# Latent attention: the order of whole and 64-row score products on TensorE

## The reference

```python
def chunk_causal_mla_attention(q_nope, q_pe, k_nope, k_pe, v):   # 8 heads, per block of 128 queries
    s = (einsum('bqhd,bkhd->bhqk', qn_b, k_nope)      # 128 features of a head
         + einsum('bqhd,bkd->bhqk', qp_b, k_pe)) * scale   # 64 rotary features, one key for all heads
    s = where(chunk_mask(q_idx, k_idx), s, finfo.min)
    p = softmax(s, axis=-1)
    return einsum('bhqk,bkhd->bqhd', p, v)

def mla_mixer(hn, kv, positions, w_q_a, q_g, w_q_b, w_o):
    q = (rmsnorm(hn @ w_q_a, q_g) @ w_q_b)            # 128 + 64 features of each head
    o = chunk_causal_mla_attention(q_nope, rope(q_pe), k_nope, k_pe, v)
    return o.reshape(B, S, -1) @ w_o
```

## Time and profile before

| | before |
|---|---|
| median of 3 runs | 936.29 us (935.82 to 936.38) |
| the profiled execution | 935.75 us |
| its span on the core | 933.7 us |
| mean granted TensorE clock | 0.998 |
| TensorE busy | 923.2 us, 99% of the span |
| VectorE busy | 668.7 us, 72% |
| ScalarE busy | 512.1 us, 55% |
| the latent attention's scores to the end of its transposes | 702 to 733 us from the span's start |

### The profile page before, as it was taken

One profiled execution on the slowest core, in us unless ns is written; L12 is line 12 of the kernel. 1 busy time (PEld: TensorE's weight loads), 2 busy tenths in 40 slices (PEclk: granted clock), 3 DMA queues, 4 the chain that ended last, 5 costly groups with the idle time before them and its releaser, 6 DMA issues.

```text
span 933.7 us, 14734 instructions
## 1 busy us (share of the span) xinstructions
PE 923.2 (99%) x5805; PEld 812.4 (87%) x5805; DVE 668.7 (72%) x867; ACT 512.1 (55%) x698; POOL 33.8 (4%) x48
## 2 busy tenths in 40 slices
PE   9999999999999999999999999999999999999996
PEld 8999988888888978899998888888998888888885
DVE  5878877889888886776668666567768576556664
ACT  6766855666665576444346444444747664444443
POOL 1200011000000000000000000001000000000000
PEclk9999999999999999999999999999999999999999
DMA  9944144656565547555546655655453555556541
GB/s 299 275 142 145 23 166 140 210 183 221 180 218 187 182 133 226 181 171 165 170 142 226 195 200 191 182 199 177 111 154 136 181 192 191 184 196 205 181 135 45
DMA packets 118736, 164.24 MB, mean 176 GB/s; under 512 B 14592, under 2 KB 96957, under 8 KB 118557
## 3 DMA queue, kind: packets, MB, share of 16 engines
q1 hardware_dynamic: 117067, 158.52, 52.6%
q0 software_dynamic: 1312, 4.68, 1.8%
q10 hardware_dynamic: 304, 0.33, 0.1%
HBM read 162.47 MB, written 1.05 MB: 175 GB/s over the span
## 4 chain that ended last, share of the span: by engine, by line
PE 96%; DVE 1%; ACT 1%; issue 0%; POOL 0%; POOLq 0%; DVEq 0%; ACTq 0%
PE ps L309 20%; PE ps L311 20%; PE ps L310 20%; PE ps L1049 19%; PE ps L1046 10%; PE ps L1561 1%; PE ps L1415 1%; PE ps L1538 1%; PE ps L588 1%; ACT w_hi L220 1%; PE ps L1530 0%; PE ps L1550 0%; DVE w_lo L233 0%; PE ps L2194 0%; PE ps L410 0%
## 5 line engine op out<-in xcount | busy, mean ns | idle before, releaser
L239 DVE TENSOR_TENSOR w_lo<-raw,w_hi 128x2048 fp32r<-128x2048 f32 (+2 forms) x145 | 328.1, 2265 | 114.3 <-ACT w_hi L223 113.9
L223 ACT ACTIVATE w_hi<-raw 128x2048 fp32r<-128x2048 f32 (+2 forms) x146 | 276.8, 1896 | 100.7 <-PE ps L311 98.2
L1049 PE MATMUL ps<-hT,w_hi 128*128 128x512 f32 x768 | 241.2, 395 | 0.0
L1046 PEld LDWEIGHTS ps<-hT,w_lo 128*128 128x128 f32 x768 | 144.0, 188 | 33.5
L309 PE MATMUL ps<-w_hi,act_hi 128*128 128x512 f32 x416 | 162.9, 392 | 0.0
L311 PE MATMUL ps<-w_lo,act_hi 128*128 128x512 f32 x416 | 162.0, 389 | 0.0
L310 PE MATMUL ps<-w_hi,act_lo 128*128 128x512 f32 x416 | 161.9, 389 | 0.0
L1046 PE MATMUL ps<-hT,w_lo 128*128 128x256 f32 x768 | 151.0, 278 | 0.0
L309 PE MATMUL ps<-hT,w_hi 128*128 128x256 f32 x432 | 124.8, 289 | 1.5 <-DVE hT L541 0.7
L310 PE MATMUL ps<-hT,w_lo 128*128 128x256 f32 x432 | 122.1, 283 | 0.0
L311 PE MATMUL ps<-hT,w_hi 128*128 128x256 f32 x432 | 122.1, 283 | 0.0
(11 more groups left out here) (343 smaller groups left out, 1010.1 us busy)
## 6 DMA issues: line engine op xcount, KB each, us to landing
raw<-in_mlp_w_dram SPq DMA_DIRECT2D x64, 1024.0 KB, 5.2
raw<-in_w_up_dram SPq DMA_DIRECT2D x22, 1024.0 KB, 5.1
raw<-in_a_w_in_dram SPq DMA_DIRECT2D x16, 1024.0 KB, 5.3
raw<-in_w_down_dram SPq DMA_DIRECT2D x11, 1024.0 KB, 4.9
raw<-in_w_in_dram SPq DMA_DIRECT2D x9, 1024.0 KB, 6.8
raw<-in_a_w_out_dram SPq DMA_DIRECT2D x8, 1024.0 KB, 4.9
raw<-in_w_out_dram SPq DMA_DIRECT2D x4, 1024.0 KB, 5.1
raw<-in_b_w_o_dram SPq DMA_DIRECT2D x4, 1024.0 KB, 4.9
```

Source lines behind the costliest of these rows:

```text
L223: nc.scalar.activation(w_hi[:, s, 0:n], raw[:, r, 0:n], ACT.Copy).then_inc(hi_ready, 1)
L239: nc.vector.tensor_tensor(w_lo[:, s, 0:n], raw[:, r, 0:n], w_hi[:, s, 0:n].bitcast(F32), ALU.subtract).then_inc(lo_ready, 1)
L1046: nc.tensor.matmul(banks[:, b + t, S:2 * S], w_l[:, k, t * P:(t + 1) * P], hT[:, k, 0, :], start=k == 0, stop=False, skip_group_check=True)
L1049: mm = nc.tensor.matmul(banks[:, b + t, :], w_h[:, k, t * P:(t + 1) * P], hT[:, k, :, :].rearrange("p x s -> p (x s)"), start=False, stop= ...
```

## The change

Among the first two groups the whole products of both stand together, and the 64-row products of both behind them. Among the last two, the outputs of the second group are put ahead of the wait for the rotary queries (`m_rq`), right behind the whole products of the third group; then come the whole products of the fourth, and the 64-row products of the third and of the fourth. No other engine's list is touched, and the same instructions are issued.

```diff
             pe.wait_ge(m_qn, 2)
             pe.wait_ge(m_rq, 2)
-            at_scores(pe, gs[0])
-            at_scores(pe, gs[1])
+            at_whole(gs[0], range(NH))
+            at_whole(gs[1], range(NH))
+            at_rows(gs[0])
+            at_rows(gs[1])
             pe.wait_ge(lo_ready, u0 + 8)
             pe.wait_ge(m_kev, 4)
             queries_pe(2, u0 + 7)
@@
             at_turn(pe, gs[1])
             pe.wait_ge(m_qn, 4)
             at_whole(gs[2], (1, 2, 3))
+            at_out(pe, gs[1])
             pe.wait_ge(m_rq, 4)
+            at_whole(gs[3], range(NH))
             at_rows(gs[2])
-            at_out(pe, gs[1])
-            at_scores(pe, gs[3])
+            at_rows(gs[3])
```

## The result

The changed kernel takes 938.47 us (median of 11 runs, 937.78 to 939.01) against 935.82 us (935.26 to 936.38, 11 runs) for the kernel before, measured side by side. The ratio is 1.0029, with a 95% interval of 1.0021 to 1.0037: slower by 2.65 us, and the whole interval lies beyond 0.2%. Forecast were 2.57 us more and 938.8 us. The profiled execution took 938.40 us, with a span of 936.4.

The account below looks back on a forecast made before the run. TensorE, busy 923.2 of 933.7 us, was taken to bound the kernel. Delays of 0.72 us (first pair) and 1.85 us (last pair) sum to 2.57 us; 936.29 + 2.57 gives about 938.8 us, range 937.8 to 939.9.

Parts of the forecast that it names:

- What bounds: Whole kernel: TensorE is busy 923.2 of 933.7 us, so nearly every delay of it becomes a delay of the end.
- First pair: First two groups: late scores delay the exponential 0.84 us; TensorE pauses about 1.0 us at the transposes, 0.72 us behind.
- Last pair: Last two groups: third group's maximum about 1.85 us late on VectorE, pausing TensorE at both projection units; 1.85 us added.
- The sum: Whole kernel: 0.72 + 1.85 = 2.57 us slower, 936.29 + 2.57, about 938.8 us.
- The switches: TensorE, between whole and 64-row products: 0.20 us each; the four that go save 0.4 to 0.8 us, 0.8 taken.
- 935.7: Both pairs: only gains of 0.4 us in the first and 0.2 us in the last are kept, 935.7 us; chance 0.04.
- 937.9: First two groups: their delay is hidden, TensorE reaches the last two 0.2 us early, 937.9 us; chance 0.12.
- 936.8 us: Last two groups: their delay is the smaller one, 0.72 - 0.2, giving 936.8 us; chance 0.04.
- rival 4: TensorE's clock falls to 1.2 GHz behind the second pause, stretching 5.95 us up to twice, 944.8 us; chance 0.03.

Follow-up runs that it names:

- the best version: Kernel before with 64-row products between both groups' whole ones, early exponential table load, third maximum ahead of first group's low half: 935.13 us against 935.67, ratio 0.9993.

## Why the prediction was right

- **What bounds.** TensorE's busy time stayed at 923.2 us and the time grew by TensorE's pauses, as the prediction took it.
- **First pair.** Forecast: transposes at 710.73, and TensorE 0.72 us late from there on. After, less the 0.08: 710.81 - 0.08 = 710.73, and the second group's transposes 715.64 - 0.08 - 714.86 = 0.70 us late. The maximum was put at 705.65 and came at 705.67. Alone, this half measured 0.8 by the stretch and 0.62 by the medians.
- **Last pair.** Forecast, with the 0.72 and the 0.08 added: outputs at 717.49 (717.46 measured), the third maximum at 722.01 (721.98), the projection at 724.46 (724.48), its second unit at 730.72 (730.70). Alone: 1.9 us by the stretch, against 1.85. Behind the second unit nothing has changed, as the prediction asked: from it to the end of the span it is 936.4 - 730.70 = 205.7 us, against 933.7 - 728.07 = 205.6.
- **The sum.** 2.57 forecast; 2.6 by the stretch, 2.65 by the medians. The projected 938.8 us (938.86 by its own sum) is 0.3 to 0.4 over the measured 938.47, because the three runs shown before had a median of 936.29 and the eleven beside the changed kernel one of 935.82.
- **The switches.** 0.8 us for four, shown by the kernel with four more. In the changed kernel the queries behind the first pair begin at 706.41 - 0.08 = 706.33 instead of 706.74, 0.41 us early for two switches, where 0.40 was forecast. These gains bring nothing at the end, since TensorE waits for others at the transposes and at the projection.
- **The rivals.** Those of 935.7, 937.9 and 936.8 us needed a cover over one of the two delays; each half alone shows that neither has one. The clock stayed at its full 2.4 GHz level through pauses of 0.9 and 1.7 us, so the fall of rival 4 did not come. The busy time by stretch of the changed kernel (the last column but two is the granted clock):

```profile
702.00:740.00 38.00, 35.20 (x241) 30.66 (x240) 27.64 (x42) 28.37 (x66) 0.00 (x0) 1.00 0.39 129
```

- **What it lacked.** The wait for the third group's banks ahead of the projection (L1818) was left out of the working. In the changed kernel it ends earlier than the wait for `at_lo(gs[1])` and costs nothing; it shows only once that one is taken away.

## What to carry to other kernels

Bundling like instructions saves their switches, but it also moves the moment at which the first group is complete; work that out for each consumer before counting what the busiest engine saves. Where a late result feeds several waits, the one with the longest pause in the trace need not be the loss: follow everything that is queued behind the late instruction on its engine, for taking away the first wait may only show the next. And a consumer's own busy time is room to move things into: 1.9 us of other work went ahead of the third group's scores for nothing, and the next 1.8 us cost all of themselves.

## What had not been expected of the hardware

Nothing in kind. One size stood out: the time at which an execution reaches the attention, with the same TensorE code ahead of it, differs by 0.5 us between the ten traces (701.77 to 702.27 us), which is as much as the best version gains by its median. Where it arises is not shown; the waits for the first weights differ between the traces too. Stretches counted from one common instruction agree with the worked-out numbers to about 0.1 us.
